# Eight products with zeros ahead of each feed-forward loop, and new distances between the operands

## What is computed

```python
def _swiglu(h, w_in, w_out):                 # four times: ffn0 to ffn3
    gate, up = jnp.split(h @ w_in, 2, axis=-1)
    return (jax.nn.silu(gate) * up) @ w_out

def conv_ffn(h, w_up, conv_w, conv_b, w_down):   # twice: conv0, conv1
    u = h @ w_up
    ...                                       # three-tap convolution over the tokens
    a, g = jnp.split(conv, 2, axis=-1)
    return (jax.nn.silu(a) * g) @ w_down
```

## Time and profile before

| | us |
|---|---|
| median of 3 runs | 1814.97 |
| lowest and highest run | 1812.74, 1818.12 |
| span of the profiled execution | 1825.6 |

### The profile page before, as it was taken

One profiled execution on the slowest core, in us unless ns is written; L12 is line 12 of the kernel. 1 busy time (PEld: TensorE's weight loads), 2 busy tenths in 40 slices (PEclk: granted clock), 3 DMA queues, 4 the chain that ended last, 5 costly groups with the idle time before them and its releaser, 6 DMA issues.

```text
span 1825.6 us, 36701 instructions
## 1 busy us (share of the span) xinstructions
PE 1757.0 (96%) x14498; PEld 1721.6 (94%) x14498; DVE 1191.0 (65%) x1765; ACT 957.9 (52%) x1100; POOL 351.8 (19%) x280
## 2 busy tenths in 40 slices
PE   7999989989999899999999999989899999989998
PEld 7999989989999899998998999988899999989998
DVE  6655589976565665556456555665487776567776
ACT  5444667775444754444345444465455455655553
POOL 2000500030004600026663000566400011020001
PEclk9999999999999999999999999999999999999999
DMA  6656323335555365543434555434245454345552
GB/s 217 209 184 243 132 96 116 116 116 186 201 187 190 111 224 190 201 144 133 138 138 148 187 188 185 173 120 154 97 162 206 165 192 139 116 162 184 185 205 92
DMA packets 45168, 298.25 MB, mean 163 GB/s; under 512 B 5024, under 2 KB 5408, under 8 KB 15920
## 3 DMA queue, kind: packets, MB, share of 16 engines
q1 hardware_dynamic: 45104, 297.38, 46.0%
HBM read 296.31 MB, written 1.05 MB: 163 GB/s over the span
## 4 chain that ended last, share of the span: by engine, by line
PE 82%; DVE 10%; ACT 4%; issue 3%; DMA 1%; POOL 0%; SPq 0%; DVEq 0%; ACTq 0%
PE wk L379 15%; PE wk L380 15%; PE wk L381 15%; PE acc L379 8%; PE acc L380 8%; PE acc L381 8%; DVE x_lo L457 1%; PE wk L391 1%; PE wk L390 1%; PE wk L389 1%; PE wk L1043 1%; DVE sumsq L690 1%; DVE x L422 1%; ACT w_hi L325 1%; DVE w_lo L351 1%
## 5 line engine op out<-in xcount | busy, mean ns | idle before, releaser
L325 ACT ACTIVATE w_hi<-raw 128x2048 fp32r<-128x2048 f32 (+5 forms) x300 | 533.3, 1787 | 406.6 <-PE wk L381 337.7
L380 PE MATMUL wk<-x_lo,w_hi 128*128 128x256 f32 x2560 | 718.3, 281 | 0.0
L379 PE MATMUL wk<-x_hi,w_hi 128*128 128x256 f32 x2208 | 627.4, 284 | 21.4 <-DVE x_lo L457 16.5
L2618 POOL TENSOR_TENSOR w_lo<-raw,w_hi 128x512 fp32r<-128x512 f32 (+1 forms) x274 | 351.0, 1315 | 1459.0 <-ACT w_hi L325 1458.9
L381 PE MATMUL wk<-x_hi,w_lo 128*128 128x256 f32 x2208 | 620.6, 281 | 0.0
L351 DVE TENSOR_TENSOR w_lo<-raw,w_hi 128x2048 fp32r<-128x2048 f32 (+2 forms) x218 | 484.1, 2222 | 169.0 <-ACT w_hi L325 168.8
L380 PEld LDWEIGHTS wk<-x_lo,w_hi 128*128 128x128 f32 x2560 | 484.3, 189 | 0.3
L379 PEld LDWEIGHTS wk<-x_hi,w_hi 128*128 128x128 f32 x2208 | 422.9, 192 | 27.6 <-DVE x_lo L457 18.8
L381 PEld LDWEIGHTS wk<-x_hi,w_lo 128*128 128x128 f32 x2208 | 419.5, 190 | 0.0
L379 PE MATMUL acc<-h_hi,w_hi 128*128 128x256 f32 x1376 | 391.3, 284 | 16.3 <-DVE h_lo L2207 4.7
L380 PE MATMUL acc<-h_lo,w_hi 128*128 128x256 f32 x1376 | 387.7, 282 | 0.0
(11 more groups left out here) (325 smaller groups left out, 2140.5 us busy)
## 6 DMA issues: line engine op xcount, KB each, us to landing
raw<-w_ffn_loop SPq DMA_DIRECT2D x120, 1024.0 KB, 4.8
raw<-w_conv_loop SPq DMA_DIRECT2D x60, 1024.0 KB, 4.8
raw<-w_mla_loop SPq DMA_DIRECT2D x18, 768.0 KB, 4.2
raw<-w_hgrn_loop SPq DMA_DIRECT2D x10, 896.0 KB, 4.5
raw<-w_ple_gate SPq DMA_DIRECT2D x8, 1024.0 KB, 4.7
raw<-w_odd_loop SPq DMA_DIRECT2D x10, 768.0 KB, 4.3
raw<-w_even_loop SPq DMA_DIRECT2D x6, 1024.0 KB, 4.8
raw<-w_odd_proj SPq DMA_DIRECT2D x6, 1024.0 KB, 4.8
```

Of the source, the lines that this page charges most:

```text
L325: nc.scalar.activation(w_hi[slot][:, 0:n], raw[slot][:, 0:n], ACT.Copy).then_inc(S("hi_ready"), 1)
L379: nc.tensor.matmul(dst, hi, a_hi, start=start, stop=False, skip_group_check=True)
L380: nc.tensor.matmul(dst, hi, a_lo, start=False, stop=False, skip_group_check=True)
L2618: last = nc.gpsimd.tensor_tensor(w_lo[slot][:, a:b], raw[slot][:, a:b], w_hi[slot][:, a:b].bitcast(F32), ALU.subtract)
```

## The change

It does two things. The buffer `zero` moves ahead of `w_hi`, with a gap of 64 bytes before it and one of 192 bytes behind it; so `w_hi`, `w_lo` and `tmp` move by 2304 bytes, and all buffers behind the old place of `zero` by 256. And `pe_ffn` has a function `settle`: PE waits for what the next turn's first product waits for, and issues eight products whose weights are the first eight tiles of the coming unit's `w_hi` and whose moving operand is 256 columns of zeros, into the bank of `wk` that the turn then writes afresh. It stands ahead of the loop in all six parts. In ffn0 the first turn is taken out of the loop and `settle` stands behind it a second time.

```diff
@@ -250,10 +250,12 @@
         ln_tok = sb("ln_tok", [P, 2 * TB])
+        sb("gap_ln_zero", [P, 16])
+        zero = sb("zero", [P, 512], F32R)
+        sb("gap_zero_w", [P, 48])
         w_hi = [sb(f"w_hi{s}", [P, SLOT_TILES * P], F32R) for s in range(SLOTS)]
         w_lo = [sb(f"w_lo{s}", [P, SLOT_TILES * P], F32R) for s in range(SLOTS)]
         tmp = sb("tmp", [P, 8, SEQ])
-        zero = sb("zero", [P, 512], F32R)
         eps = sb("eps", [P, 1])
@@ -768,12 +770,30 @@
             up(first, 0, 0, opening=True)
             pe_clear_acc(pe, name).then_inc(S("acc_cleared"), 1)
             pe.wait_ge(S("acc_cleared"), ffn_index[name] + 1)
-            with pe.Fori(0, NJ - 1) as j:
+
+            def body(j):
                 up(loop, j, j + 1)
                 pe.wait_ge(S("h_lo_ready"), 2 * j + (2 * n0 + 1))
                 use_tiles(pe, loop, j, 32, out_tiles(2)[:KD], "half_out_used", 39)
                 pe.wait_ge(S("h_lo_ready"), 2 * j + (2 * n0 + 2))
                 use_tiles(pe, loop, j, 40, out_tiles(2)[KD:])
+
+            def settle(j):
+
+                need(pe, "up_read", 2 * (n0 + j) + 1)
+                slot, turn = stream_at(loop, j, 0)
+                pe.wait_ge(S(f"lo_ready{slot}"), turn + 1)
+                for n in range(8):
+                    nc.tensor.matmul(wk[:, 0, 0:SEQ], w_hi[slot][:, n * P:n * P + P], zero[:, 0:SEQ], start=True, stop=True,
+                                     skip_group_check=True)
+
+            settle(0)
+            peeled = 1 if name == phases[0][1] else 0
+            if peeled:
+                body(0)
+                settle(1)
+            with pe.Fori(0, NJ - 1 - peeled) as j:
+                body(j + peeled)
             pe.wait_ge(S("h_lo_ready"), 2 * (n0 + NJ) - 1)
```

## The result

The changed kernel is slower. Its median over 20 runs is 1831.15 us (1812.16 to 1846.6), beside 1816.59 us (1802.92 to 1831.03) for 20 runs of the kernel before on the same chip; the ratio is 1.0067, with a 95% interval of 1.004 to 1.0094, which is about 12 us. The medians lie 14.6 us apart; the ratio leaves out the two longest runs of the changed kernel (1841.6 and 1846.6 us), which count as slow ones. I had predicted 1796 us and given slower a chance of 0.23; the measured time lies 0.15 us above the upper end of the range. The lines of `channel_tile` are L381 to L383 in the changed kernel (L379 to L381 before), the clearing products L414, the products with zeros L787.

The account below looks back on a forecast made before the run. TensorE was taken to bound the kernel at 2.4 GHz. From 1825.6 us, -24.7 (loop pitch) and +5.5 (eight products) gave 1806.4 us profiled; as a median, 1815.0 - 19.2 = 1796 us, range 1757 to 1831.

Parts of the forecast that it names:

- The reading of the profile: Six feed-forward loops: TensorE sets the time, at pitches of 113.4 or 117.8 ns, two stable states chosen at a gap.
- slower settled state: Rival: at 320 bytes the state settled after the zeros is the slow one; 1834 us, up to 1841; chance 0.17.
- better than both states: Rival: at 320 bytes the streams hardly meet, pitch near 110 ns in all loops; 1767 us, down to 1750; chance 0.17.
- the reading of the token tiles: Token tiles, at 448 bytes, show 280 ns a product, near the slow kind's 281; taken as another distance, nearly slow alone.
- Part 1: Pitch in the six loops: all go to 113.4 ns, 5616 products in the slow loops gain 4.4 ns each, -24.7 us.
- The base of the sum: Profiled execution of 1825.6 us, 10.6 us above the runs' median of 1815.0; that difference was kept for the forecast.
- Part 2: The eight products: seven blocks, ffn0's first covered by a wait, the other six 48 x 115 ns, +5.5 us.
- Parts 3 and 4: Faster PE meets no other engine, 3.2 us to spare in conv loops; 256-column products outside the loops change by 0.
- distances do nothing, and the state is left to chance: Rival: the blocks cost 6 us and each loop is in either state as now; 1820 us, chance 0.13.
- the sum's 1806.4 us: Forecast for the profiled execution: 1825.6 - 24.7 + 5.5 us, before the difference to the median was kept.

Follow-up runs that it names:

- e1: Changed kernel without the eight zero products, only the buffers moved (weights 320 bytes behind the moving operands): 1820.16 us, ratio 0.9985 to the kernel before.
- e8: Changed kernel with the zeros at 0 instead of 192 bytes from the weights, products still at 320: 1806.81 us, ratio 0.9894 to the kernel before.
- e9: The changed kernel unedited, run again on the chip of the kernel with zeros at 0 and products at 320: 1824.71 us, ratio 1.0014 to the kernel before.
- e4: The changed kernel unedited, timed once more beside the kernel before on another chip: 1829.49 us, ratio 1.0085.
- e2: Changed kernel with a longer gap ahead of the zeros: zeros stay at 192, products at 64 bytes: 1829.43 us, ratio 1.0025 to the kernel before.
- e5: Changed kernel with no gap behind the zeros: zeros at 0 from the weights, products at 64: 1805.58 us, ratio 0.9923 to the kernel before.
- e6: Changed kernel with the zeros 72 bytes from the weights, products at 64: 1807.04 us, ratio 0.9921 to the kernel before.
- e3: Changed kernel with other gaps, zeros 64 bytes from the weights and products at 64: 1810.95 us, ratio 0.9996 to the kernel before.
- m4: Bare kernel, products at 64, zeros' distance set by shifting their weights, sixteen trials a case: 15 fast without zeros, 11, 8, 11, 14 with 4, 8, 16, 24 at 64.
- m6: Bare kernel, products at 64, zeros moved instead of their weights, sixteen trials a case: eight zeros fast in 16 at 0, 10 at 64, 7 at 192.

## Why the prediction was wrong, point by point

**The reading of the profile held.** TensorE bounds the kernel, two pitches exist at an equal clock, they are chosen at a gap and stay until the next: in all eleven profiles of networks each loop keeps its mean over every 200 products within 0.2 ns from end to end. No loop changed in between, which the prediction had named as what would refute it. The cause is two streams that disturb one another; the bare kernels show it by the address alone.

**The addresses were worked out by the wrong modulus.** I counted modulo 512. The pitch repeats after 256 bytes, so that a move by 256 is none, and e1 shows no difference in time. The rivals that priced 320 as a distance of its own (slower settled state; better than both states) fall with it, and so does the reading of the token tiles: their 448 is 192 modulo 256, where the bare kernel shows both pitches, three trials of twelve at the lower.

**Part 1 is the step that failed: "the one into which a fixed start can bring all of them", -24.7 us.** It rested on no row, only on the wish that a fixed start would mean a fixed and a fast end. Its size for a loop was right (1440 x 4.4 ns = 6.3 us; e8 and e9 differ by 17.9 us in the median with the same instructions). What was wrong is that eight zeros at 192 fix it. They leave 54% of the starts slow, where 29% are slow without them in the bare kernel and, by the medians, about 2.4 of 6 loops in the network before. In place of -24.7 us stands a cost: 0.54 - 0.29 = 0.25 more slow loops for each of six by the bare shares, 1.5 x 6.4 us = 9.6 us. With the blocks' 4.7 us (below) that makes 14 us, where 12 (by the ratio) and 14.6 (by the medians) were measured. That these agree so well is in part luck, since the comparisons themselves differ. The medians of the result give 4.1 - 2.4 = 1.7 more slow loops (worked out from the measured times, so it can't confirm them). By the same estimate the medians give 4.1, 3.8 and 3.1 slow loops for the changed kernel in its three comparisons (the result, e4, e9) and 3.8 for e2, and 2.4, 2.1, 4.1 and 3.5 for the kernel before beside them. So with zeros at 192 half of the loops or more are slow each time, while the share of the kernel before differs from one comparison to the next: in two the zeros add 1.7 slow loops, in the others 0.3 and -1.0. That such zeros always make things worse is not shown; that they don't help is.

A start that fixes the end does exist, and it is at another distance of the zeros: e5, e6 and e8 have what part 1 promised, with 0.1 to 0.3 slow loops in a run by the medians. The form of the change was sound, its one number was not.

**The base of the sum was wrong as well.** I took the 10.6 us between the profiled execution and the median for a constant of profiling. The only constant is 1.8 us, and it goes the other way: a run is that much longer than its span. The profiled execution was itself one of the longer ones, of some 1827 us, with four slow loops where the average has 2.4. Had all six been made fast, the gain over the average run would have been 2.4 loops, 15 us, less the blocks, and not 24.7. The better kernels bear this out: e5 lies 16 us below the kernel before on its chip, with the blocks' cost in it, and e8 20.5 us on a chip where the kernel before had 1827.33. As a span with all loops fast, the sum's 1806.4 us was right: e3, e5, e6 and e8 have 1801.8 to 1807.6 us. Taking 10.6 us off it made a time that no run of any kernel here came near; the shortest of all was 1801.37 us.

**Part 2 was a little too large.** 0.72 us a block and not 0.92, since 0.33 us of the time between the clearing and the first product is hidden by the block's earlier start; five such are 3.6 us. In ffn0 the first block is covered, as priced, and the second turn's first product came at 46.60 us and not at 45.48 us, 1.1 us later, behind a block that began at 45.59 us. In all 4.7 us against 5.5; the spans less their slow products differ by 4 us with and without blocks.

**Parts 3 and 4.** No new wait stands in a loop of any profile, fast as all six are in e5: the cover of 3.2 us held. Outside the slow loops a profile has 2089 to 2673 slow products, a spread worth 2.6 us with no order by layout: nothing, as taken.

**The rivals.** The one that came nearest is "distances do nothing, and the state is left to chance", at 1820 us and 0.13. It had the blocks' cost and chance right; what it missed is that chance has a share, which without blocks differs between comparisons, and that zeros at other distances take it away. The comparison of after is one draw from this: the three comparisons gave 1.0067, 1.0085 and 1.0014, so the changed kernel is slower than the one before in two and not to be told from it in the third.

**What stays open.** Why 52, 64, 76 and 88 bytes, and their mirror images, have the pitch of 113.3 ns at all. Why zeros at 0 and 72 always lead into it in the network and those at 192 half the time. Why zeros at 64, which by the median left about one slow loop in a run of e3, were fast in only 8 (m4) and 10 (m6) of 16 bare trials. Why 76 gave 120.0 ns in two loops of one network and in none of 32 trials. That the share of slow loops in the kernel before differs from chip to chip (medians of 1814.5 to 1827.3 us) was seen and not explained.

**A better kernel than both** is the changed one with the zeros at distance 0 (e5, e8) or 72 (e6): 0.8 to 1.1% faster than the kernel before, and its runs (12, 6 and 12 of them) spread over 7 to 10 us where those of the kernel before (17 to 29) spread over 20 to 28.

## What to carry to other kernels

Where one instruction has two durations in one trace at an equal clock, and each holds from gap to gap, a profile is one draw: count the slow stretches in several, and compare medians of many runs before a sum starts from one of them. Work put ahead of a stretch can choose its state, but only a measurement says which distance does; one that imitates the seam exactly (here which of the two operands was moved) agreed with the network, and one that did not pointed the wrong way. A term that says "this can bring all of them to the better state" is a hope until a row shows such a start and its end, and belongs beside its opposite at even chances.

## What the runs showed of the hardware

- Products of 256 columns, with a load of 128 columns for each, start 113.3 to 121.3 ns apart at full clock, by the distance between weights and moving operand modulo 256 bytes.
- At 64 bytes there are two pitches, 113.3 and 117.8 ns. Each held for more than 1400 products.
- Products that themselves run at 118 to 120 ns can leave the ones behind them at 113.3 ns in 14 of 14 cases (zeros at 0 in e5 and e8), and blocks that ran at 113 ns (seen in ffn2 of e4 and the second block of e2) were followed by a slow loop.
- In bare trials without zeros the first step is a hint: at distances 64 and 320, 220 or 221 ns went on fast in 37 of 39, 225 or 226 ns slow in 14 of 14, and 222 ns either way.
